# Projection and expert weights loaded a stage earlier, and the projection stage's token tiles interleaved

## The chip, the cores and the metric

The kernel runs on one NeuronCore of a Trainium2 chip. The metric is device time in microseconds from the launch's first to its last instruction; the median of several runs counts. The engines are TensorE (PE, matmuls; its weight loads are PEld), VectorE (DVE), ScalarE (ACT) and GpSimd (POOL); SP, ACT and POOL each issue transfers on a queue of their own, and all queues share 16 DMA engines. TensorE's clock is granted at one of two levels, 1.2 or 2.4 GHz; the profile writes 0.50 and 1.00.

## The reference

One decoder layer over 1024 prompt rows and 8 sequences of 8 sample rows, all in float32, width 1024:

```python
mod = jax.nn.silu(c) @ w_ada + b_ada
shift1, scale1, gate1, shift2, scale2, gate2 = jnp.split(mod[:, None, :], 6, axis=-1)
h = rmsnorm(x, norm1_g) * (1 + scale1) + shift1
aq, ak, av, mqk, mv, mo, mi, mf = jnp.split(h @ w_in, SPLITS, axis=-1)
...  # attention on aq, ak, av; short conv on mqk, then mLSTM with a carried state
mix = jnp.concatenate([hA.reshape(B, T, W_A), att.reshape(B, T, W_B)], axis=-1).astype(x.dtype) @ w_out
x = x + gate1 * mix
h2 = rmsnorm(x, norm2_g) * (1 + scale2) + shift2
x = x + gate2 * peer(h2, peer_wq, peer_keys, peer_u, peer_v)
```

`peer` scores 2 x 128 sub-keys per head, takes the 16 best experts of each of 8 heads for a row (128 picks), and sums their one-neuron outputs: u and v rows of 1024 values, gathered from a table of 16384.

## The kernel before

Three stages, each a block in which every engine has its own program; semaphores order them, and an all-engine barrier stands between stages. There is no scheduler: each engine runs its instructions in the order in which the code writes them, and an engine that waits holds back all behind it.

**Stage 0** makes the modulation rows: 12 loads of w_ada (2 MB each, two buffers, on SP's queue), 8 matmuls each, plus two tables of position biases (the second, s_bias, is written out by SP at the end). The rows go to a scratch tensor `mod_rows`.

**Stage 1** is the projection stage. Its weight w_in (14.7 MB) fills the memory from END_SMALL to END_W. Nine tiles: eight of 128 prompt rows and one of 64 sample rows. Engine programs call `tile(i, ...)` for tile 0, then in a hardware loop (Fori) for tiles 1 to 7, then for the sample tile. On TensorE a tile is: transposes of the normed rows h (L564), gates (8 columns), mqk (64 matmuls, L572), mv, two small sums of the gates (tri, all), mo, a_rep (L585), the three diag matmuls that end in m_rep (L588 to L590), the attention's q and k, scores s_ps (L598), key transposes ktok (L601), the attention's v (av), num (L613, L614), and cup, the update of the carried state (L619). Column matmuls over w_in go through `project`, so they all carry L556. Between them DVE and ACT make: x's mean square (ACT L490) and h (DVE L665, L666); the gates' log (lf); the short conv (32 DVE instructions); diag_a, diag_m, arg; decay and carry (ACT, L518, L521); og, scores, q_carry, kws (DVE, to L742), the norm of q and k (to L753, its mean square by ACT), hid and its norm, the state. POOL stores q, k, v and hid of a tile (hid to `mix_rows`, L456). ACT begins the stage by issuing w_in's eight loads and sixteen copies of 4 MB each from the old caches to the output, DRAM to DRAM:

```python
for k in range(KD):
    act.dma_start(w_in[:, k], ins["w_in"][:, k]).then_inc(sig["w_in_in"], 16)
for b in range(DB):
    for name in ("k_s", "v_s"):
        act.dma_start(outs[name][b, 0:WBUF - DS], ins["cache_" + name[0]][b, DS:WBUF]).then_inc(sig["cache_out"], 16)
```

SP meanwhile loads two mod rows, spread over 128 partitions, and then x tile by tile. Before the sample tile it reloads mod, stores the prompt's state and fetches the sample's conv_tail; after it, it stores the sample's state, and the stage ends when that has landed.

**Stage 3** first runs a sample window: attention of the 64 sample rows over the cached keys and values (POOL loads keys_t and vals), interleaved with the attention, output projection (w_out) and expert search (w_q) of prompt tile 0. SP issues the loads of w_out (4 MB) and w_q (8 MB) at that window's start. Then come nine windows of expert picks: POOL gathers one expert row per partition and pick (L1104), DVE takes the dot product, ACT the gate, TensorE the weighted sum, while the next tile's search runs between picks.

Of the kernel before, what the change touches and what calls it, by code (L numbers as in the profile page):

```python
# [19 lines left out]
P = 128  # L20
D = 1024
# [175 lines left out]
PER_P, PER_S = 59, 59  # L197
END_KEPT = W_B + N_KEPT


def layer(nc, ins, outs):

    with ExitStack() as ctx:
# [31 lines left out]
def stage0(nc, block, sig, mem, psum, const, table, ins, scratch):  # L235
# [8 lines left out]
    rows = mem[:, END_SMALL:END_SMALL + 6 * D]  # L244
    tab = mem[:, END_SMALL + 6 * D:END_SMALL + 6 * D + LTAB]
    s_part = Region(mem, END_SMALL + 6 * D + LTAB, END_W)
# [7 lines left out]
    def _(sp):  # L254
# [4 lines left out]
        for n in range(N_ADA):  # L259
# [3 lines left out]
            sp.dma_start(w[:, n % 2], ins["w_ada"][:, :, cols]).then_inc(sig[f"ada_in{n % 2}"], 16)  # L263
# [9 lines left out]
        sp.wait_ge(sig["s_bias_tab"], len(S_PIECES))  # L273
        sp.dma_start(scratch["s_bias"].ap(), s_tab).then_inc(sig["tables_out"], 16)
        sp.wait_ge(sig["tables_out"], 48)

    @block.scalar
    def _(act):
# [8 lines left out]
        nc.scalar.activation(cond, cond, ACT.Silu).then_inc(sig["cond"], 1)  # L287
        act.wait_ge(sig["small_in"], 80)
# [46 lines left out]
def stage1(nc, block, sig, mem, psum, const, ins, outs, scratch):  # L335

    w_in = mem[:, END_SMALL:END_W].rearrange("p (k n) -> p k n", k=KD)
# [30 lines left out]
    s_state = work.take(DB, H_A, DK + 1)  # L368
# [36 lines left out]
    def _(sp):  # L405
# [8 lines left out]
        with sp.Fori(1, NT) as i:  # L414
            tile(i, P, ins["x"][bass.ds(i * P, P), :])
# [23 lines left out]
        sp.dma_start(outs["m_s"], sm["mnew"][0:NS]).then_inc(sig["out1"], 16)  # L439
        sp.wait_ge(sig["s_state"], DB)  # L440
# [4 lines left out]
    def _(pool):  # L445
# [17 lines left out]
        with pool.Fori(1, NT) as i:  # L463
            store(i, P, bass.ds(i * P, P), bass.ds(i * P + WBUF - SEQ, P))
# [6 lines left out]
    def _(act):  # L471
        for k in range(KD):
            act.dma_start(w_in[:, k], ins["w_in"][:, k]).then_inc(sig["w_in_in"], 16)

# [5 lines left out]
        def tile(i, rows, kind, per):  # L480
            chain = Chain(act, sig["act1"], i * per)
# [6 lines left out]
            act.wait_ge(sig["x_in"], (i + 1) * 16)  # L488
            act.wait_ge(sig["h"], i)
            chain.link(nc.scalar.activation(squares[0:rows], x[0:rows], ACT.Square, accum_out=xss[0:rows]))  # L490
            inv_rms(xrs[0:rows], xln[0:rows], xss[0:rows], D, "x_rms")
            act.wait_ge(sig["h_t_ps"], i + 1)
            act.wait_ge(sig["av_ps"], i)
            for half in range(2):
                src = psum[:, half].rearrange("p (k t) -> p k t", k=4)[:, :, 0:rows]
                cp = nc.scalar.activation(h_t[:, 4 * half:4 * half + 4, 0:rows], src, ACT.Copy)  # L496
                cp.then_inc(sig["h_t"], 1)

# [3 lines left out]
            nc.scalar.activation(sm["soft"][0:rows], sm["soft"][0:rows], ACT.Ln, bias=1.0).then_inc(sig["soft"], 1)  # L502

# [9 lines left out]
            nc.scalar.activation(conv[:, :, 0:rows], conv_y[:, :, 0:rows], ACT.Silu).then_inc(sig["silu"], 1)  # L513

# [28 lines left out]
            assert chain.n == per, chain.n  # L543

        tile(0, P, "p", 7)
        with act.Fori(1, NT) as i:
            tile(i, P, "p", 7)
        tile(NT, NS, "s", 7)

    @block.tensor  # L550
    def _(pe):
        ident, ones = const["ident"], const["ones"]

        def project(bank, col, n, rows, at=0):
            for k in range(KD):
                mm = nc.tensor.matmul(psum[0:rows, bank, at:at + n], h_t[:, k, 0:rows], w_in[:, k, col:col + n], start=k == 0, stop=k == KD - 1)  # L556
            return mm

        def tile(i, rows, kind):
# [5 lines left out]
            tr.then_inc(sig["h_t_ps"], 1)  # L565
            pe.wait_ge(sig["h_t"], 2 * i + 2)
            pe.wait_ge(sig["w_in_in"], 16 * KD)
            pe.wait_ge(sig["mnew"], i)
            project(7, O_G, 2 * H_A, rows).then_inc(sig["gates_ps"], 1)
            for c in range(8):  # L570
                for k in range(KD):
                    mm = nc.tensor.matmul(psum[:, c // 4, c % 4 * P:c % 4 * P + rows], w_in[:, k, O_QK + c * P:O_QK + (c + 1) * P],  # L572
                                          h_t[:, k, 0:rows], start=k == 0, stop=k == KD - 1)
            mm.then_inc(sig["mqk_ps"], 1)
            pe.wait_ge(sig["scores"], i)
            project(5, O_MV, W_A, rows).then_inc(sig["mv_ps"], 1)
# [4 lines left out]
            project(6, O_MO, W_A, rows).then_inc(sig["mo_ps"], 1)  # L581

            pe.wait_ge(sig["diag_a"], i + 1)
            pe.wait_ge(sig["state"], i)
            nc.tensor.matmul(psum[0:rows, 2, 0:H_A * rows], ones[0:rows, 0:rows], diag_a_of(rows), start=True, stop=True).then_inc(sig["a_rep"], 1)  # L585
            pe.wait_ge(sig["diag_m"], i + 1)
            pe.wait_ge(sig["av"], i)
            nc.tensor.matmul(psum[0:rows, 3, 0:H_A * rows], ones[0:rows, 0:rows], diag_m_of(rows), start=True, stop=True)  # L588
# [3 lines left out]
            project(2, 0, W_B, rows)  # L592
# [1071 lines left out]
```

## Time and profile before

| | before |
|---|---|
| median of 3 runs | 4375.03 us (4374.49 to 4392.1) |
| profiled execution | 4374.66 us, span 4373.0 us |
| mean granted clock | 0.918 |
| PE busy | 3560.7 us, 81% |
| DVE busy | 2393.2 us, 55% |
| ACT busy | 1640.2 us, 38% |
| POOL busy | 1279.2 us, 29% |
| DMA | 1419.95 MB, mean 325 GB/s |

All numbers on rows are from the profiled execution. Busy shares are averages over stages with different limits, so they don't tell what bounds a stage; for that one goes by stretch, and in a stretch by the wait that ends last. A row of the timeline gives the start, the time and, in brackets, how long the engine had been idle and what released it. A float32 matmul shows as two instructions (x16 for eight matmuls).

### The profile page before, as it was taken

How to read it: one execution, taken by the hardware profiler on the slowest of the kernel's cores; microseconds unless marked ns; L12 is line 12 of the kernel's file. 1: busy time of each engine (PE TensorE's matmuls, PEld its weight loads, DVE VectorE, ACT ScalarE, POOL GpSimd, SP SyncE). 2: the span in 40 equal slices, each digit the busy share in tenths (PEclk: the TensorE clock that was granted, in tenths of full speed). 3: DMA queues.
4: the chain of work that ended last, by engine and by line, in shares of the span. 5: the costliest groups of instructions: out<-in, count | busy, mean ns of one | idle time of the engine just before them, and what ended most of it. 6: DMA issues, size and time to landing. Idle time of an engine off the chain costs nothing.

```text
span 4373.0 us, 38660 instructions
## 1 busy us (share of the span) xinstructions
PE 3560.7 (81%) x12228; PEld 1818.6 (42%) x12228; DVE 2393.2 (55%) x5587; ACT 1640.2 (38%) x4396; POOL 1279.2 (29%) x1204
## 2 busy tenths in 40 slices
PE   7288788684867987997898898789799888989877
PEld 1054454453533533443453444445345344524321
DVE  1033433322464784595486468449646845947844
ACT  0022322311335335435434533543453354334333
POOL 0000000000223343343343334234334434435433
PEclk9688888865989999999999899999999999999999
DMA  6897100146669999999999899999999999999998
GB/s 237 301 338 252 38 19 19 43 23 262 237 236 372 400 415 358 403 411 391 372 414 416 329 394 413 360 387 410 413 376 390 410 394 395 397 374 401 411 408 368
DMA packets 251979, 1419.95 MB, mean 325 GB/s; under 512 B 42963, under 2 KB 65875, under 8 KB 105603
## 3 DMA queue, kind: packets, MB, share of 16 engines
q0 software_dynamic: 168768, 1200.70, 68.4%
q1 hardware_dynamic: 79588, 132.71, 9.8%
q10 hardware_dynamic: 3440, 84.35, 5.5%
q8 instruction: 84, 1.38, 0.1%
q14 instruction: 99, 0.81, 0.1%
HBM read 1385.48 MB, written 98.73 MB: 339 GB/s over the span
## 4 chain that ended last, share of the span: by engine, by line
PE 30%; DMA 24%; DVE 11%; ACT 8%; issue 2%; POOL 0%; SPq 0%; ACTq 0%; POOLq 0%; DVEq 0%
DMA mem<-in_experts,mem 21%; PE psum L1279 20%; DVE mem L1573 6%; PE psum L1196 3%; PE psum L1178 3%; DMA mem<-key_cols 2%; ACT L1383 2%; DVE mem L1439 1%; ACT mem L1387 1%; DVE mem L1438 1%; ACT mem L1384 1%; ACT L1306 1%; PE psum L1134 1%; ACT mem L1306 1%; ACT mem L1383 1%
## 5 line engine op out<-in xcount | busy, mean ns | idle before, releaser
L1279 PE MATMUL psum<-mem 128*128 128x512 f32 (+1 forms) x4352 | 2141.1, 626 | 387.9 <-ACT mem L1387 386.4
L1104 POOL DMA_INDIRECT mem<-in_experts,mem x1088 | 1213.3, 1115 | 1872.9 <-PE psum L1279 1804.2
L1573 DVE CUSTOM_DVE_ANT_0 mem<-mem 128x1024 f32<-128x1024 f32 x1088 | 1322.8, 1222 | 708.5 <-DMA mem<-in_experts,mem 695.7
L1279 PEld LDWEIGHTS psum<-mem 128*128 128x128 f32 (+1 forms) x4352 | 776.8, 193 | 1471.1 <-ACT mem L1387 747.7
L1383 ACT ACTIVATE mem<-mem 128x1 f32<-128x1 f32 x1088 | 219.2, 201 | 1562.9 <-DVE mem L1573 1560.2
L1387 ACT ACTIVATE mem<-mem 128x128 f32<-128x128 f32 (+1 forms) x1088 | 433.3, 398 | 35.6
L556 PE MATMUL psum<-mem 128*128 128x512 f32 (+3 forms) x864 | 351.2, 558 | 10.2 <-ACT mem L496 10.2
L1384 ACT ACTIVATE mem<-mem 128x1 f32<-128x1 f32 x1088 | 320.4, 295 | 35.3
L1196 PEld LDWEIGHTS psum<-mem 128*128 128x128 f32 x2304 | 274.4, 191 | 45.2 <-issue 41.8
L1196 PE MATMUL psum<-mem 128*128 128x128 f32 (+1 forms) x2304 | 282.1, 276 | 2.5 <-ACT mem L1335 2.5
L556 PEld LDWEIGHTS psum<-mem 128*128 128x128 f32 (+1 forms) x864 | 159.7, 207 | 176.7 <-issue 162.9
L449 POOL DMA_DIRECT2D qkv_rows<-mem x9 | 5.1, 563 | 742.1 <-ACT mem L534 742.1
L564 PE MATMUL psum<-mem 128*128 128x128 f32 (+1 forms) x72 | 16.9, 415 | 192.0 <-DVE mem L666 192.0
L572 PE MATMUL psum<-mem 128*128 128x128 f32 (+1 forms) x1152 | 158.9, 310 | 0.0
L572 PEld LDWEIGHTS psum<-mem 128*128 128x128 f32 x1152 | 157.8, 226 | 0.0
L1416 DVE CUSTOM_DVE_ANT_0 mem<-psum,mem 128x128 f32<-128x128 f32 (+7 forms) x64 | 48.4, 756 | 192.7 <-PE psum L1136 166.0
L1438 DVE MAX8 mem<-mem 128x8 f32<-128x128 f32 (+3 forms) x432 | 145.8, 338 | 12.5
L1439 DVE FIND_INDEX8 mem<-mem 128x8 uint32<-128x128 f32 (+3 forms) x432 | 141.9, 328 | 0.0
L1178 PE MATMUL psum<-mem 128*128 128x512 f32 (+1 forms) x288 | 135.5, 595 | 0.0
L1134 PE MATMUL psum<-mem 64*128 64x512 f32 (+3 forms) x160 | 67.9, 531 | 56.3 <-DMA mem<-key_cols 56.2
L303 PE MATMUL psum<-mem 128*9 128x512 f32 x192 | 91.7, 637 | 20.0 <-DMA mem<-in_b_ada 13.9
L1383 ACT ACT_TABLE_LOAD x80 | 102.6, 1283 | 14.0 <-DVE mem L1573 12.6
(255 smaller groups left out, 2612.4 us busy)
## 6 DMA issues: line engine op xcount, KB each, us to landing
out_k_s<-in_cache_k ACTq DMA_DIRECT2D x8, 4080.0 KB, 125.1
out_v_s<-in_cache_v ACTq DMA_DIRECT2D x8, 4080.0 KB, 137.4
mem<-in_w_ada SPq DMA_DIRECT2D x12, 2048.0 KB
mem<-mod_rows SPq DMA_DIRECT2D x34, 512.0 KB
mem<-in_experts,mem POOLq DMA_INDIRECT x1088, 9.7
mem<-in_keys_t POOLq DMA_DIRECT2D x16, 1024.0 KB, 6.8
mem<-in_vals POOLq DMA_DIRECT2D x16, 1024.0 KB, 8.4
mem<-in_w_in ACTq DMA_DIRECT2D x8, 1796.0 KB, 24.8
```

Of the source, the lines that this page charges most:

```text
L556: mm = nc.tensor.matmul(psum[0:rows, bank, at:at + n], h_t[:, k, 0:rows], w_in[:, k, col:col + n], start=k == 0, stop=k == KD - 1)
L572: mm = nc.tensor.matmul(psum[:, c // 4, c % 4 * P:c % 4 * P + rows], w_in[:, k, O_QK + c * P:O_QK + (c + 1) * P], h_t[:, k, 0:rows], start ...
L1104: pool.indirect_dma_start(out=ring[:, g % N_SLOTS].rearrange("p a n -> p (a n)"), out_offset=None, in_=ins["experts"][:, :], in_offset=bas ...
L1178: mm = nc.tensor.matmul(psum[0:r, out_banks(n)[half]], turned[:, k, 0:r], w_out[:, k, half * 512:(half + 1) * 512], start=k == 0, stop=k = ...
L1196: mm = nc.tensor.matmul(psum[:, 5, j % 4 * P:j % 4 * P + r], w_q[:, k, j * NKEY:(j + 1) * NKEY], turned[:, k, 0:r], start=k == 0, stop=k = ...
L1279: mm = nc.tensor.matmul(psum[0:r, half], diag[:, g % 4, 0:r], ring[:, g % N_SLOTS, 1, half * 512:(half + 1) * 512], start=c == 0, stop=c = ...
L1383: chain.link(a.activation(act_v[:, c:c + 1], dots[:, c:c + 1], ACT.Gelu))
L1384: chain.link(a.activation(weight[:, c:c + 1], act_v[:, c:c + 1], ACT.Copy, scale=gate[i % 2][:, c:c + 1]))
L1387: a.activation(diag[:, g % 4, 0:r], spread, ACT.Copy, scale=weight[:, c:c + 1]).then_inc(sig["diag"], 1)
L1438: chain.link(v.max(values[:, e:e + 8], src))
L1439: chain.step(v.max_index(places[:, e:e + 8], values[:, e:e + 8], src))
L1573: v.tensor_tensor_reduce(row, row, h2[i % 2], 1.0, 0.0, ALU.mult, ALU.add, dots[:, c:c + 1]).then_inc(sig["dots"], 1)
```

## The change

Five things, in one kernel:

- w_in is loaded in stage 0 by ACT, six of its eight parts at once, two after the s_bias table has left the memory that they fill. Stage 0's own tables move behind END_W for it, and ACT, not SP, writes s_bias out. The semaphore w_in_in is kept over the barrier.
- w_ada is laid out chunk by chunk, so that a load reads 16 KB in a row for each partition instead of eight times 2 KB.
- In stage 1 the hardware loops are unrolled, and tile i+1's mean square, norm, transposes and copy to h_t are written inside tile i (`rows_rms`, `normed`, `turn`, `turned`), with a second h_t in the room of the sample's state. TensorE's order in a tile is changed.
- At the end of stage 1, SP loads w_out and w_q into w_in's place as soon as its last matmul is done, ahead of the store of the sample's state. Stage 3 loads them no more.
- Stage 3's buffers are laid out anew for that; a small copy (s_kt) is made in two parts.

```diff
-        sig.retire()
+        sig.retire(keep=("w_in_in",))
...
-        sig.retire(keep=("cache_out",))
+        sig.retire(keep=("cache_out", "w_out_in", "w_q_in"))
...
-            sp.dma_start(w[:, n % 2], ins["w_ada"][:, :, cols]).then_inc(sig[f"ada_in{n % 2}"], 16)
+            sp.dma_start(w[:, n % 2], ins["w_ada"][n]).then_inc(sig[f"ada_in{n % 2}"], 16)
...
+        for k in range(6):
+            act.dma_start(w_in[:, k], ins["w_in"][:, k]).then_inc(sig["w_in_in"], 16)
+        act.wait_ge(sig["s_bias_tab"], len(S_PIECES))
+        act.dma_start(scratch["s_bias"].ap(), s_tab).then_inc(sig["s_bias_out"], 16)
+        act.wait_ge(sig["s_bias_out"], 16)
+        act.wait_ge(sig["s_bias_ps"], len(S_PIECES))
+        for k in range(6, KD):
+            act.dma_start(w_in[:, k], ins["w_in"][:, k]).then_inc(sig["w_in_in"], 16)
...
+    def weights_in(sp):
+
+        w_out, w_q = last_weights(mem)
+        sp.wait_ge(sig["av_ps"], NT + 1)
+        sp.dma_start(w_out, ins["w_out"]).then_inc(sig["w_out_in"], 16)
+        sp.dma_start(w_q, ins["w_q"]).then_inc(sig["w_q_in"], 16)
...
         sp.dma_start(outs["m_s"], sm["mnew"][0:NS]).then_inc(sig["out1"], 16)
+        weights_in(sp)
         sp.wait_ge(sig["s_state"], DB)
...
-        for k in range(KD):
-            act.dma_start(w_in[:, k], ins["w_in"][:, k]).then_inc(sig["w_in_in"], 16)
-
+        act.wait_ge(sig["w_in_in"], 16 * KD)
...
+            if i < NT:
+                rows_rms(i + 1, P if i + 1 < NT else NS)
...
+            if i < NT:
+                turned(i + 1, P if i + 1 < NT else NS)
...
-            pe.wait_ge(sig["hraw"], i)
-            pe.wait_ge(sig["kws"], i)
+            if i >= 1:
+                pe.wait_ge(sig["ext"], i)
             for k in range(KD):
                 tr = nc.tensor.transpose(psum[:, k // 4, k % 4 * P:k % 4 * P + rows], h[0:rows, k * P:(k + 1) * P], ident[0:rows, 0:rows])
...
+            if i < NT:
+                turn(i + 1, P if i + 1 < NT else NS)
+            if i >= 1:
+                pe.wait_ge(sig["state"], i)
+            project(i, 2, 0, W_B, rows)
...
+            if i + 1 < NT:
+                normed(i + 1, P)
+            if i + 1 == NT:
+                dve.wait_ge(sig["mod_in"], 64)
+                normed(NT, NS)
...
-        dve.wait_ge(sig["mod_in"], 64)
         dve.wait_ge(sig["s_conv_in"], 16 * 8)
...
-                sp.dma_start(w_out, ins["w_out"]).then_inc(sig["w_out_in"], 16)
...
-                sp.dma_start(w_q, ins["w_q"]).then_inc(sig["w_q_in"], 16)
```

What stands where now is shown at three places. First TensorE in a prompt tile, in the program before; L564 are the transposes, L556 the projections (8 columns are the gates), L572 mqk, L579 and L580 the gates' sums, L585 a_rep, L588 to L590 the diag matmuls:

```order
L564 MATMUL psum<-mem 128x128 x8
L556 MATMUL psum<-mem 128x8 x8
L572 MATMUL psum<-mem 128x128 x64
L556 MATMUL psum<-mem 128x512 x8
L579 MATMUL psum<-mem 128x4
L580 MATMUL psum<-mem 128x4
L556 MATMUL psum<-mem 128x512 x8
L585 MATMUL psum<-mem 128x512
L588 MATMUL psum<-mem 128x512
L589 MATMUL psum<-mem 128x512
L590 MATMUL psum<-mem 128x4
L556 MATMUL psum<-mem 128x512 x16
```

The tile began with its own transposes, and q and k (the last row) followed the diag matmuls. The same place in the changed program, where L589 are the projections, L616 mqk, L598 the transposes, L633 a_rep, L638 to L640 the diag matmuls:

```order
L589 MATMUL psum<-mem 128x8 x8
L589 MATMUL psum<-mem 128x512 x8
L616 MATMUL psum<-mem 128x128 x64
L621 MATMUL psum<-mem 128x4
L622 MATMUL psum<-mem 128x4
L589 MATMUL psum<-mem 128x512 x8
L598 MATMUL psum<-mem 128x128 x8
L589 MATMUL psum<-mem 128x512 x8
L633 MATMUL psum<-mem 128x512
L589 MATMUL psum<-mem 128x512 x8
L638 MATMUL psum<-mem 128x512
L639 MATMUL psum<-mem 128x512
```

mv stands ahead of mqk, the transposes in the middle are the next tile's, and q and k stand ahead of the diag matmuls, one on either side of a_rep.

Second, ACT around the barrier between stages 0 and 1 (L225) in the program before:

```order
L285 DMA mem<-in_s_onehot 128x3864
L287 ACT_TABLE_LOAD
L287 ACTIVATE mem<-mem 128x72
L225 UNCONDITIONAL_BRANCH
L470 UNCONDITIONAL_BRANCH
L473 DMA mem<-in_w_in 128x3592 x8
L477 DMA out_k_s<-in_cache_k 64x16320
```

And in the changed one (the barrier is L230):

```order
L289 DMA mem<-in_s_onehot 128x3864
L291 ACT_TABLE_LOAD
L291 ACTIVATE mem<-mem 128x72
L293 DMA mem<-in_w_in 128x3592 x6
L295 DMA s_bias_rows<-mem 128x1288
L299 DMA mem<-in_w_in 128x3592 x2
L230 UNCONDITIONAL_BRANCH
L492 UNCONDITIONAL_BRANCH
L497 DMA out_k_s<-in_cache_k 64x16320
```

The cache copies are now the first that ACT issues in stage 1.

Third, SP at the end of stage 1 in the changed program:

```order
L458 DMA out_conv_s<-mem 128x8x3 x8
L460 DMA out_m_s<-mem 64x4
L353 DMA mem<-in_w_out 128x8192
L354 DMA mem<-in_w_q 128x16384
L463 DMA out_state_s<-mem 128x4128
```

The two weights stand between the small store m_s and the state's store; before, the state's store followed m_s, and the weights came in stage 3 behind the store of the key columns.

## Rows read from the trace of the kernel before

**Rows 1.** Busy us of each engine by stretch; last columns: PEclk, DMA share, GB/s.

```profile
0.00:146.30 146.30, 103.58 (x220) 21.66 (x220) 15.34 (x24) 1.55 (x2) 0.23 (x5) 0.91 0.62 213
1013.50:1266.90 253.40, 172.63 (x1096) 106.33 (x1096) 108.90 (x391) 73.24 (x154) 43.16 (x73) 0.82 0.66 239
1266.90:4373.00 3106.10, 2658.28 (x8264) 1276.49 (x8264) 1967.04 (x4446) 1348.31 (x3852) 1213.33 (x1088) 0.96 0.98 392
```

**Rows 2.** First and last copy issue on ACT, and all sixteen copies' landing.

```profile
150.99 0.63 ACTq L477 DMA_DIRECT2D out_k_s<-in_cache_k  x1
184.94 20.13 ACTq L477 DMA_DIRECT2D out_v_s<-in_cache_v  x1
DMA to landing us min/median/max: 49.0/130.7/216.1
```

**Rows 3.** TensorE's timeline: start, us, line, work, count, [idle before it <- releaser].

```profile
281.33 1.06 PE L619 MATMUL psum<-mem 128*128 128x129 f32 x8
376.54 1.97 PE L564 MATMUL psum<-mem 128*128 128x128 f32 x8 [12.10 <-DVE mem L666]
379.69 3.58 PE L556 MATMUL psum<-mem 128*128 128x8 f32 x16 [1.18 <-ACT mem L496]
417.97 2.08 PE L588 MATMUL psum<-mem 128*128 128x512 f32 x2 [3.43 <-DVE mem L714]
421.48 13.98 PE L556 MATMUL psum<-mem 128*128 128x512 f32 x32
```

**Rows 4.** Stretches of the second and the ninth tile, columns as before.

```profile
294.00:301.00 7.00, 5.43 (x25) 5.03 (x25) 0.34 (x1) 1.08 (x2) 0.00 (x0) 0.50 0.99 325
301.00:318.00 17.00, 17.00 (x131) 16.68 (x132) 0.84 (x3) 1.90 (x4) 0.00 (x0) 0.88 1.02 351
340.00:362.00 22.00, 22.00 (x64) 10.60 (x63) 10.62 (x12) 6.18 (x13) 0.00 (x0) 1.00 1.01 344
890.00:918.00 28.00, 28.00 (x134) 27.90 (x133) 0.31 (x2) 1.90 (x4) 0.00 (x0) 0.50 0.00 1
```

**Rows 5.** Timeline of ACT, then of DVE, behind the third tile's m_rep.

```profile
423.96 0.57 ACT L521 ACTIVATE mem<-psum 128x512 f32<-128x512 f32 x1
426.50 0.69 DVE L725 TENSOR_TENSOR mem<-mem 128x512 f32<-128x512 f32 x1
436.46 0.69 DVE L729 TENSOR_TENSOR mem<-psum,mem 128x512 f32<-128x512 f32 x1 [9.27 <-PE psum L598]
442.74 1.23 DVE L753 TENSOR_TENSOR mem<-mem 128x1024 f32<-128x1024 f32 x1
```

**Rows 6.** Landing of x asked at 212.4 and 458.6, and of mix_rows at 289.3.

```profile
DMA to landing us min/median/max: 27.8/27.8/27.8
DMA to landing us min/median/max: 3.6/3.6/3.6
DMA to landing us min/median/max: 62.7/62.7/62.7
```

**Rows 7.** What ended TensorE's idle time on the modulation matmuls (us, times).

```profile
  DMA mem<-in_b_ada: 24.9, 7
```

**Rows 8.** Timeline of TensorE, DVE and TensorE around the ninth tile.

```profile
854.87 1.06 PE L619 MATMUL psum<-mem 128*128 128x129 f32 x8
884.28 1.28 DVE L665 SCALAR_TENSOR_TENSOR mem<-mem 64x1024 f32<-64x1024 f32 x1 [19.98 <-DMA mem<-in_conv_tail]
955.73 7.08 PE L556 MATMUL psum<-mem 128*64 128x512 f32 x16
```

**Rows 9.** Chain that ended last (sample window), and the page on vals.

```profile
1029.56 13.00 DMA mem<-in_keys_t
1045.75 25.15 DMA mem<-in_vals
1150.58 5.30 DMA mem<-in_keys_t
mem<-in_vals POOLq DMA_DIRECT2D x16, 1024.0 KB, 8.4
```

More of the change, by code:

```diff
@@ L243, in stage0 @@
     rel = work.take(H_B)
-    rows = mem[:, END_SMALL:END_SMALL + 6 * D]
-    tab = mem[:, END_SMALL + 6 * D:END_SMALL + 6 * D + LTAB]
-    s_part = Region(mem, END_SMALL + 6 * D + LTAB, END_W)
+    rows = work.take(6 * D)
+    tab = work.take(LTAB)
+    w_in = mem[:, END_SMALL:END_W].rearrange("p (k n) -> p k n", k=KD)
+    s_part = Region(mem, END_SMALL + 6 * W_IN, END_W)
     s_hot, s_rel, s_tab = s_part.take(3, COLS), s_part.take(3, P), s_part.take(COLS)
@@ L413, in _ @@
         tile(0, P, ins["x"][0:P, :])
-        with sp.Fori(1, NT) as i:
-            tile(i, P, ins["x"][bass.ds(i * P, P), :])
+        for i in range(1, NT):
+            tile(i, P, ins["x"][i * P:(i + 1) * P, :])
         sp.wait_ge(sig["h"], NT)
@@ L478, in _, with rows_rms, turned, tile @@
         lnscale, eps = const["lnscale"], const["eps"]
-        def tile(i, rows, kind, per):
-            chain = Chain(act, sig["act1"], i * per)
+        chain = Chain(act, sig["act1"])
+        def rows_rms(i, rows):
+            act.wait_ge(sig["x_in"], (i + 1) * 16)
+            act.wait_ge(sig["h"], i)
+            if i >= 2:
+                act.wait_ge(sig["qss"], i - 1)
+            chain.link(nc.scalar.activation(squares[0:rows], x[0:rows], ACT.Square, accum_out=xss[0:rows]))
+            chain.link(nc.scalar.activation(xln[0:rows], xss[0:rows], ACT.Ln, scale=1.0 / D, bias=eps[0:rows]))
+            nc.scalar.activation(xrs[0:rows], xln[0:rows], ACT.Exp, scale=-0.5).then_inc(sig["x_rms"], 1)
+        def turned(i, rows):
+            act.wait_ge(sig["h_t_ps"], i + 1)
+            if i >= 2:
+                act.wait_ge(sig["av_ps"], i - 1)
+            for half in range(2):
+                src = psum[:, half].rearrange("p (k t) -> p k t", k=4)[:, :, 0:rows]
+                cp = nc.scalar.activation(h_ts[i % 2][:, 4 * half:4 * half + 4, 0:rows], src, ACT.Copy)
+                cp.then_inc(sig["h_t"], 1)
+        def tile(i, rows, kind):
             def inv_rms(out, tmp, total, n, event):
@@ L486, in inv_rms @@
                 nc.scalar.activation(out, tmp, ACT.Exp, scale=-0.5).then_inc(sig[event], 1)
[L488 to L497, printed above, removed]
             act.wait_ge(sig["gates"], i + 1)
@@ L542, in tile @@
             inv_rms(sm["hrs"][0:rows], sm["hln"][0:rows], sm["hss"][0:rows], DK, "h_rms")
[L543 to L548, printed above, removed]
+        rows_rms(0, P)
+        turned(0, P)
+        for i in range(NT):
+            tile(i, P, "p")
+        tile(NT, NS, "s")
     @block.tensor
@@ L565, in tile @@
             tr.then_inc(sig["h_t_ps"], 1)
+        def tile(i, rows, kind):
             pe.wait_ge(sig["h_t"], 2 * i + 2)
-            pe.wait_ge(sig["w_in_in"], 16 * KD)
-            pe.wait_ge(sig["mnew"], i)
-            project(7, O_G, 2 * H_A, rows).then_inc(sig["gates_ps"], 1)
+            if i == 0:
+                pe.wait_ge(sig["w_in_in"], 16 * KD)
+            else:
+                pe.wait_ge(sig["mnew"], i)
+            project(i, 7, O_G, 2 * H_A, rows).then_inc(sig["gates_ps"], 1)
+            if i >= 1:
+                pe.wait_ge(sig["scores"], i)
+            project(i, 5, O_MV, W_A, rows).then_inc(sig["mv_ps"], 1)
+            if i >= 1:
+                pe.wait_ge(sig["hraw"], i)
+                pe.wait_ge(sig["kws"], i)
             for c in range(8):
@@ L620, in tile @@
                 mm.then_inc(sig["cup"], 1)
-        tile(0, P, "p")
-        with pe.Fori(1, NT) as i:
+        turn(0, P)
+        for i in range(NT):
             tile(i, P, "p")
@@ L653, in _, with normed, tile @@
         taps = const["conv"]
-        def tile(i, rows, kind, per):
-            chain = Chain(dve, sig["dve1"], dve_base + i * per)
+        def normed(i, rows):
+            R = slice(0, rows)
+            dve.wait_ge(sig["x_rms"], i + 1)
+            if i >= 1:
+                dve.wait_ge(sig["h_t_ps"], i)
+            chain.link(v.scalar_tensor_tensor(out=h[R], in0=x[R], scalar=xrs[R], in1=mod[R, 1], op0=ALU.mult, op1=ALU.mult))
+            v.tensor_tensor(h[R], h[R], mod[R, 0], ALU.add).then_inc(sig["h"], 1)
+        def tile(i, rows, kind):
             R = slice(0, rows)
@@ L719, in tile @@
             chain.wait()
[L720 removed]
+            v.tensor_tensor(arg_of(rows), bc(const[kind + "_negT"][R], 1, H_A), heads_ps(1, rows, rows), ALU.subtract).then_inc(sig["arg"], 1)
             dve.wait_ge(sig["og"], i + 1)
@@ L779, in tile @@
                 v.tensor_tensor(state[:, 2:4], state[:, 2:4], num_ps(P, 1, (2, 3)), ALU.add).then_inc(sig["state"], 1)
-            assert chain.n == per, (kind, chain.n)
         v.memset(state, 0.0).then_inc(sig["dve1"], 1)
```

118 lines of the change are left out of this document (60 added, 58 removed).

## The prediction, on record before the changed kernel ran

> **What bounds the kernel now.** I read first the busy time of each engine by stretch [rows 1]. The modulation rows fill it to 146.3, the projection stage (eight prompt tiles, then a ninth of 64 sample rows) to 1013.5, the sample window of the expert stage to 1266.9, and 3106.1 us of expert picks the rest. In the picks the DMA engines are 98% busy at 392 GB/s: gathers bound them, and the edit moves no instruction there, so I carry them over unchanged. All that can be won lies in the first 1267 us, where a different thing ends last in each stretch.
>
> Then I read ACT's timeline behind 146.3 [rows 2]. It issues eight loads of w_in and sixteen cache copies; the last issue alone takes 20.13 us and ends at 205.07, 58.8 us into the stage. The first Square on x stands behind it, and norm, transposes and all matmuls behind that. So ACT's full issue queue holds back the stage's start.
>
> Next the TensorE timeline of a prompt tile [rows 3]. From the end of tile 0 (281.33 + 1.06 = 282.39) to that of tile 7 (854.87 + 1.06 = 855.93) seven tiles take 573.5 us, 81.93 each. TensorE stands still three times in one: 12.10 us before the transposes, 1.18 before the gates, 3.43 before diag_m; the rest, 65.2 us, is matmuls. The granted clock [rows 4] is 0.50 just after the long wait, 0.88 over the following 17 us, 1.00 late in the tile: the wait costs twice.
>
> **The tile loop, the largest term.** The new order puts tile i+1's norm, transposes and copies inside tile i, so that the 12.10 and 1.18 go. What is TensorE's work then? Transposes (1.97 us) and gates (3.43 us from 379.69 to 383.12) run at 0.50; at 1.00 they would take half, 2.7 less. The 17 us at 0.88 hold 17 x 0.12 / 0.5 = 4.1 us at half clock, 2.0 too much. diag_m and its neighbours take 3.5 us (417.97 to 421.48) for four passes of 512 columns; 32 such passes take 13.98, so 0.44 each, and 1.5 are lost. That leaves 65.2 - 6.2 = 59.0 us.
>
> What is late next is the chain DVE - ACT - DVE after m_rep, the last of the diag matmuls (421.48). Before, both q/k projections, the 13.98 us, stood behind m_rep and covered it; now they stand ahead of it, and only s_ps, the key transposes, av and num do. ACT's decay and carry end at 424.53, 3.1 us after m_rep [rows 5]; TensorE has 1.4 us for s_ps and the key transposes, so it stands 1.7 in two waits, for arg and for carry. DVE needs 5.7 us for arg and og (to 427.19), then, with no gap left in between, 7.5 for scores, q_carry, kws, the sum of squares, ACT's Ln and Exp, and the q/k norm (436.46 to 443.97): 13.2 in all. TensorE is at cup, which overwrites q and k, after 3.1 + 7.0 of av + 1.8 of num = 11.9, and stands 1.3. So 3.0 us of waits, and 62.0 per tile. Waits this short may still cost clock: the one of 3.43 us does (the 1.5 above). I take 65; bounds 62 (no loss) and 68 (all cold parts stay: 65.2 + 3.0). Seven tiles at 65 instead of 81.93 are -118.5, tile 0 gains about 1 from the order. Sum **-119** (-140 to -98).
>
> **The start of the stage.** With w_in already in memory, ACT's issues fit the queue sooner: sixteen at about 0.65 us are 10 us, and the last may wait for the first copy to land; 20 us, before 58.8. But what shares the DMA engines with what changes too. Before, the two mod rows (shift and scale, spread over 128 partitions) and the first x, three transfers of 512 KB on SP's queue, ran beside w_in and were there long before ACT was free. Now they run beside the copies from the first moment. The trace shows what that costs: x of tile 1, fetched while copies ran, landed after 27.8 us, that of tile 4, after the copies, in 3.6 [rows 6]. So 512 KB beside copies takes about 22 us once started (27.8 less some 5 of start and landing); three in line on one queue take 66, bounds 3 x 3.6 and 3 x 27.8. The first x lands some 70 us into the stage; Square, norm and transposes follow as before. 70 instead of 58.8: **+11** (-39 if only ACT's queue counts, +25).
>
> The last copy landed 216.1 us after its issue at 184.94, at 401, the first at 150.99 + 49.0 = 200 [rows 2]: 13.4 us each, 215 in all, so they still run in tile 1. There DVE waits, before it overwrites hid, for POOL's store of tile 0's hid, which took 62.7 us to land among the copies [rows 6]. It is issued some 7 us after tile 0's cup and needed 61.5 us after it: **+8** (0 to +10), once. In a tile of 82 us this was covered.
>
> **The modulation stage.** w_ada comes in 16 KB pieces per partition instead of 2 KB. TensorE waited there 24.9 us in seven waits that end with a load's last part [rows 7], the start among them. Against that, 10.8 MB of w_in now share the DMA engines with the first five loads and 3.6 MB with loads 6 and 7: at the 400 GB/s of the picks 36 us of transfer, in a stage whose DMA share is 0.62. The two about cancel. At the end s_bias no longer leaves on SP after the last row: 2 us. I take **-2** (-15 if the waits go, +8 if w_in delays the loads).
>
> **The sample tile.** Its norm waited for DVE, and DVE for the conv_tail loads, 19.98 us after its last step on the prompt state [rows 8]; TensorE stood meanwhile and then ran 28 us at 0.50 [rows 4]. From tile 7's end (855.93) to the end of av (955.73 + 7.08 = 962.81) are 106.9 us. Now x, h and the transposes are done in tile 7, so gates, mv and mqk run in those 20 us. What is late next is the same conv_tail, before DVE adds the gate bias: 8.4 us for the state + 20 + 2.4 for ACT and DVE = 30.7 until lf. Then mo at part clock (9), q (7), a_rep (0.6), k (7), diag_m, s_ps, transposes and waits (5), av (7) and two small steps: 67 to 68 us. **-39** (-41 to -30). The rest of the tile, 50 us, keeps its work. Into it come 12.6 MB of w_out and w_q, on SP's queue ahead of the state's store, which is needed 42 us after av and closes the stage. At the 392 GB/s of the picks the weights need 32 us: covered, with 10 to spare; at half that rate the end would come 22 us late.
>
> **The sample window.** In the chain that ended last, the third keys_t load took 13.00 us and the first vals 25.15, while w_out and w_q were loading; the same kind later takes 5.30, and the median of vals is 8.4 [rows 9]. 7.7 + 16.7 go: **-25** (-10 to -30; the bias rows that follow on SP's queue may be late next).
>
> Sum: -119 + 11 + 8 - 2 - 39 - 25 = -166. The profiled execution took 4374.66 us, its span 4373.0; the median of the runs is 4375.03, so no allowance is needed. 4374.7 - 166 = **4209 us**.
>
> **Rivals.** (1) x is not held up by copies and the stage starts when ACT is free: 4209 - 50 = 4159. For it: SP asks first. Against it: the landing of 27.8 us. (2) The queues take turns in larger parts, so that each of the three transfers waits for one copy of 13.4 us: x after 44 us, 4209 - 26 = 4183. Against it: a lone x would then need 13.4 + 3.6 = 17 us, the row shows 27.8. The Trainium skill (DMA: Bandwidth & Descriptors, Queues, rings and completion order) says that a DMA engine drains a whole packet of descriptors from one queue before it turns to the next; by that rule this rival would hold, and the landing here does not agree with it. (3) The tile stays at 70: cold parts remain, or another wait joins; 4209 + 7 x 5 = 4244. (4) The overlap fails, because some wait keeps one tile behind the other, and the period stays 82: 4328. Against it: no wait in the new order needs the end of the tile before, but for hraw and kws, both ready within 2 us of it. (5) Slower: TensorE never leaves the half clock in the tile loop, since no stretch of it is free of waits. Work of 59.0 us becomes 118, the period 121, the time 4209 + 7 x 56 = 4601. It turns slower than before from a period of 65 + 166/7 = 88.7. For it: in the ninth tile 64-column matmuls ran 28 us at 0.50 without a gap [rows 4]. Against it: with 128 and 512 columns every tile reaches 1.00 within some 10 us.
>
> **How the numbers follow.** Forecast 0.52, (1) 0.12, (2) 0.08, (3) 0.19, (4) 0.05, (5) 0.04. The forecast's own range is 4185 to 4235. Rivals (2) and (3) lie near it and belong to the range, (1) too; 4145 to 4258 leaves out about 0.2: (4), (5) and the tails. A difference under 0.5% (22 us) I count as none. Faster 0.94: all but (5) and part of (4); same 0.02; slower 0.04.
>
> **What would show it.** Right: a period of 62 to 69 us from cup to cup with granted clock above 0.95; the first x landing some 70 us into the stage, with ACT idle before it; one longer tile, the second; the ninth tile without the 31 us wait; the window from s_raw to the first gather near 228 us; the picks within 5 us of 3106. Wrong: ACT's issues ending last at the start; a TensorE wait above 3 us in each tile; the stage's end waiting for the state's store; picks that have changed.

## The result and the profile after

| | before | after |
|---|---|---|
| median of the runs, us | 4380.3 (4 runs, 4374.5 to 4392.1) | 4180.7 (4 runs, 4171.3 to 4189.1) |
| ratio, 95% interval | | 0.954 (0.951 to 0.957) |
| profiled execution, us | 4374.7 | 4189.1 (span 4187.3) |

The kernel became 4.6% faster, 200 us; 4209 was forecast, 28 us too much, with 4145 to 4258 as the range; it lies 4 us below the forecast's own 4185 to 4235. The two profiled executions differ by 185.7 us of span. By stage, before and after:

| from, to | before | after | measured | forecast |
|---|---|---|---|---|
| modulation stage | 146.3 | 146.0 | -0.3 | -2 |
| its end to the first Square | 58.9 | 54.2 | -4.7 | +11 |
| first transpose to tile 7's end | 643.6 | 509.5 | -134.1 | -119 + 8 |
| tile 7's end to the end of av in tile 9 | 106.9 | 66.7 | -40.2 | -39 |
| end of av to the expert stage | 50.7 | 52.3 | +1.6 | 0 |
| sample window | 253.5 | 231.8 | -21.6 | -25 |
| picks | 3106.1 | 3119.8 | +13.7 | 0 |

Between the first Square and the first transpose lie 7 us in both.

First the busy time of each engine by stretch of the kernel after, cut at the same events as [rows 1] (the columns are those of [rows 1]):

```profile
146.00:207.20 61.20, 0.00 (x0) 0.00 (x0) 3.06 (x6) 4.21 (x6) 0.31 (x1) 0.50 0.99 333
207.20:716.60 509.40, 485.07 (x2248) 310.67 (x2248) 254.40 (x602) 166.01 (x318) 18.43 (x32) 0.98 0.39 134
716.60:835.60 119.00, 88.74 (x402) 57.96 (x400) 42.25 (x120) 22.54 (x48) 3.66 (x7) 0.74 0.82 166
835.60:1067.40 231.80, 174.33 (x1096) 106.87 (x1096) 109.30 (x391) 73.43 (x155) 43.18 (x73) 0.84 0.58 207
1067.40:4187.30 3119.90, 2655.81 (x8264) 1274.90 (x8264) 1967.58 (x4446) 1348.69 (x3852) 1218.03 (x1088) 0.96 0.98 390
```

In the tile loop TensorE is busy 485 of 509 us at a granted clock of 0.98. Ahead of it lie 61 us in which it does nothing while the DMA engines are busy 0.99: that is now the longest standstill ahead of the picks. ACT's timeline there answers to [rows 2]:

```profile
146.03 0.66 ACTq L497 DMA_DIRECT2D out_k_s<-in_cache_k  x1
...
156.29 9.84 ACTq L497 DMA_DIRECT2D out_v_s<-in_cache_v  x1
200.18 1.06 ACT L508 ACTIVATE mem<-mem 128x1024 f32<-128x1024 f32 x1 [193.35 <-DMA mem<-in_x]
```

The last of the sixteen issues ends at 166.13, and ACT then waits 34 us more, for x. What ended last at the stage's start was ACT's queue and is now a DMA. TensorE's timeline of one tile in the middle of the loop answers to [rows 3]:

```profile
530.42 1.13 PE L667 MATMUL psum<-mem 128*128 128x129 f32 x8 [1.15 <-DVE mem L811]
...
580.29 0.66 PE L649 MATMUL psum<-mem 128*128 128x128 f32 x4 [0.18 <-DVE mem L778]
582.08 7.13 PE L589 MATMUL psum<-mem 128*128 128x512 f32 x16 [1.13 <-ACT mem L554]
...
592.15 1.02 PE L667 MATMUL psum<-mem 128*128 128x129 f32 x7 [1.15 <-DVE mem L811]
```

From cup to cup are 61.73 us. Three waits are left, for arg, for carry and ahead of cup for the q/k norm, 2.5 us together; the waits of 12.10 and 3.43 us are gone. One stretch differs. These are rows of DVE at the end of tile 1, whose last steps reach into tile 2, then of TensorE:

```profile
334.63 1.23 DVE L808 TENSOR_TENSOR mem<-psum,mem 128x1024 f32<-128x1024 f32 x1 [2.64 <-DMA out_v_p<-mem]
348.05 0.23 DVE L817 COPY mem<-psum 128x2 f32<-128x2 f32 x2 [10.94 <-DMA mix_rows<-mem]
```
```profile
337.26 1.13 PE L667 MATMUL psum<-mem 128*128 128x129 f32 x8 [1.89 <-DVE mem L811]
349.74 2.62 PE L616 MATMUL psum<-mem 128*128 128x128 f32 x15 [2.69 <-DVE mem L823]
```

DVE waits for tile 0's stores of v and of hid (the latter issued at 282.36, so 65.7 us in landing), and TensorE for DVE. Tiles 1 to 3 take 62.47, 66.33 and 65.09 us, 8.7 more than three others. But tile 3 has no wait beyond the usual three. These rows are the first 10 us or so of it, then tile 3 and tile 4 as windows:

```profile
405.00:415.00 10.00, 10.00 (x26) 5.48 (x26) 3.16 (x8) 6.71 (x17) 0.87 (x2) 0.66 0.39 149
403.60:468.70 65.10, 62.63 (x281) 39.67 (x281) 32.20 (x76) 21.18 (x41) 2.14 (x4) 0.95 0.09 33
468.70:530.40 61.70, 59.25 (x280) 37.92 (x281) 32.20 (x76) 21.19 (x41) 2.14 (x4) 1.00 0.10 35
```

TensorE's work takes 62.6 us in place of 59.3, at a granted clock of 0.95: right behind the two waits of 1.1 us at the end of tile 2 the clock fell to its lower level for some 7 us (an estimate: 10 us at 0.66). So 3.4 of the 8.7 us are clock, and no store. In the ninth tile the gap answers to [rows 8]:

```profile
724.60 14.51 PE L616 MATMUL psum<-mem 128*128 128x64 f32 x128
748.17 0.37 PE L621 MATMUL psum<-mem 64*64 64x4 f32 x2 [9.07 <-DVE mem L722]
...
776.29 7.08 PE L589 MATMUL psum<-mem 128*64 128x512 f32 x16 [0.74 <-ACT mem L554]
```

TensorE does gates, mv and mqk while conv_tail lands and then stands 9.07 us. In the sample window the chain that ended last reads, in answer to [rows 9]:

```profile
853.29 4.32 DMA mem<-in_keys_t
859.75 9.20 DMA mem<-in_vals
...
877.96 7.66 DMA mem<-bias_rows
899.13 7.28 DMA mem<-in_keys_t
```

The loads of 13.00 and 25.15 us are back to what they take elsewhere, and the bias rows come next.

### The profile page after: what moved, and what is told of

It is laid out like the page before. It is cut to its first block, busy times and chain, and to the rows that moved or that the text cites. A ratio compares the mean times of both kernels' runs of the same rounds, so it can differ in the third digit from the quotient of the medians.

```text
span 4187.3 us, 38259 instructions
## 1 busy us (share of the span) xinstructions
PE 3507.9 (84%) x12228; PEld 1772.0 (42%) x12228; DVE 2391.9 (57%) x5587; ACT 1616.4 (39%) x4381; POOL 1283.8 (31%) x1204
## 4 chain that ended last, share of the span: by engine, by line
PE 32%; DMA 25%; DVE 11%; ACT 8%; issue 2%; POOL 1%; SPq 0%; ACTq 0%; POOLq 0%; DVEq 0%
PE psum L1335 21%; DMA mem<-in_experts,mem 20%; DVE mem L1631 6%; PE psum L1252 4%; PE psum L1234 3%; DMA mem<-key_cols 3%; ACT L1441 2%; DVE mem L1497 1%; ACT mem L1445 1%; DVE mem L1496 1%; ACT mem L1442 1%; DMA mem<-qkv_rows 1%; ACT L1362 1%; PE psum L1190 1%; ACT mem L1441 1%
## 5 line engine op out<-in xcount | busy, mean ns | idle before, releaser
L1335 PEld LDWEIGHTS psum<-mem 128*128 128x128 f32 (+1 forms) x4352 | 774.5, 193 | 1458.0 <-ACT mem L1445 733.4
L589 PE MATMUL psum<-mem 128*128 128x512 f32 (+3 forms) x864 | 342.7, 548 | 11.0 <-ACT mem L554 9.8
L1252 PEld LDWEIGHTS psum<-mem 128*128 128x128 f32 x2304 | 274.4, 191 | 45.1 <-issue 41.7
L1252 PE MATMUL psum<-mem 128*128 128x128 f32 (+1 forms) x2304 | 282.1, 275 | 2.5 <-ACT mem L1391 2.5
L589 PEld LDWEIGHTS psum<-mem 128*128 128x128 f32 (+1 forms) x864 | 148.8, 190 | 178.4 <-issue 164.6
L616 PEld LDWEIGHTS psum<-mem 128*128 128x128 f32 x1152 | 131.5, 194 | 7.7 <-issue 4.2
L616 PE MATMUL psum<-mem 128*128 128x128 f32 (+1 forms) x1152 | 131.9, 276 | 2.7 <-DVE mem L823 2.7
L508 ACT ACTIVATE mem<-mem 128x1024 f32<-128x1024 f32 (+1 forms) x9 | 9.4, 1045 | 212.4 <-DMA mem<-in_x 212.4
```

The costliest lines, as they stand in the source:

```text
L589: mm = nc.tensor.matmul(psum[0:rows, bank, at:at + n], h_ts[i % 2][:, k, 0:rows], w_in[:, k, col:col + n], start=k == 0, stop=k == KD - 1)
L1252: mm = nc.tensor.matmul(psum[:, 5, j % 4 * P:j % 4 * P + r], w_q[:, k, j * NKEY:(j + 1) * NKEY], turned[:, k, 0:r], start=k == 0, stop=k = ...
L1335: mm = nc.tensor.matmul(psum[0:r, half], diag[:, g % 4, 0:r], ring[:, g % N_SLOTS, 1, half * 512:(half + 1) * 512], start=c == 0, stop=c = ...
```

## Experiments

Twelve kernels were run. All but one change a few lines of the changed kernel ("after" below: 4180.7 us, first gather at 1067.5). Since the picks differ from execution to execution (see the section on why), the time of the first gather is given too, which leaves them out.

**Each half by itself.** In weights_only the weights load ahead and the tile loop is that of before.

> All three weights are loaded ahead of time, but the projection stage's tile loop is that of the kernel before (no overlap of tiles, q and k projected behind the diag matmuls). My theory: the two halves add up. The start gives 4.7 us, the sample window 21.6, the loop nothing: 4380 - 26 = 4354, and the overlap's share is the other 173 of the 200 us. Rival: with w_in out of the way the copies lie beside the old tiles in another way, and the parts don't add up: more than 10 us off that number.

Measured: 4354.3 us, 0.995 (0.993 to 0.997) of before, which was 4373.6 in the runs beside it, so 19 us less (12 to 31 by the interval); first gather at 1236.3, 30.6 sooner than before. The seven tiles as windows:

```profile
278.00:851.40 573.40, 456.42 (x1963) 298.82 (x1961) 227.33 (x532) 169.51 (x301) 17.53 (x31) 0.85 0.22 77
```

They take 573.4 us, as before, at the same clock of 0.85. So the weights are worth some 20 to 30 of the 200 us and the overlap the other 170 to 180. Within the 10 us that the rival names, the parts add up.

**The weights of the expert stage.** u_wlast:

```diff
-        weights_in(sp)
...
+                sp.dma_start(w_out, ins["w_out"]).then_inc(sig["w_out_in"], 16)
...
+                sp.dma_start(w_q, ins["w_q"]).then_inc(sig["w_q_in"], 16)
```

> The loads of w_out and w_q go back to the start of the expert stage. My theory: the sample window returns from 231.8 to 253.5 us and the piece from the end of av to the stage's end gets 1.6 shorter: +20, 4201. Rival: the window got shorter from something else that the change moved (a different state of the DMA queues), and the loads are hidden either way: within 5 us of 4181.

Measured: 4203.8 us, 23 above after; ratio 0.962 (0.959 to 0.964); first gather at 1084.4, 17 later, as its tiles 1 to 3 happen to be 6.3 us shorter. The window takes 254.6 us, and its chain has the long loads again:

```profile
845.82 13.33 DMA mem<-in_keys_t
862.34 25.70 DMA mem<-in_vals
```

With the weights out of the window they are 4.32 and 9.20. The theory holds, and the rival falls.

**The weights of the projection stage.** u_win:

```diff
-        for k in range(6):
-            act.dma_start(w_in[:, k], ins["w_in"][:, k]).then_inc(sig["w_in_in"], 16)
...
-        act.wait_ge(sig["w_in_in"], 16 * KD)
+        for k in range(KD):
+            act.dma_start(w_in[:, k], ins["w_in"][:, k]).then_inc(sig["w_in_in"], 16)
```

> The loads of w_in go back to the start of the projection stage, ahead of the cache copies; all else is as in the changed kernel. My theory: what ends last at that start is whichever transfer shares the DMA engines with the first x or fills ACT's issue queue, so w_in ahead of time only changes places with the copies. The first Square then runs some 59 us into the stage, as it did before the change, in place of 54; the modulation stage is 0 to 5 us shorter without w_in's 14 MB; total within 8 us of the changed kernel's 4181. Rival: w_in's 36 us of transfer (14.4 MB at the 400 GB/s of the picks) were really taken out of the stage's start, and come back: 4210 or more.

Measured: 4174.5 us, ratio 0.953 (0.949 to 0.956): no difference from after that these runs can tell. ACT's timeline:

```profile
133.99 4.49 ACTq L489 DMA_DIRECT2D mem<-in_w_in  x8
...
173.22 16.12 ACTq L492 DMA_DIRECT2D out_v_s<-in_cache_v  x1
189.45 1.06 ACT L503 ACTIVATE mem<-mem 128x1024 f32<-128x1024 f32 x1 [182.71 <-issue]
```

The first Square waits for ACT's issues again, 55.5 us into the stage, but the stage begins at 134.0 in place of 146.0: without w_in beside them the loads of w_ada make TensorE wait 24.6 us in the modulation stage, with it 33.5. So w_in ahead costs 12 us in the modulation stage, more than the 5 expected, and at the start of the next the copies take its place. TensorE starts 10.7 us sooner than in after, but its eight tiles take 8.5 us more in this profile, and the first gather, at 1064.9, is only 2.6 sooner.

**The copies out of the way.** copies_spread issues two copies in each tile, behind the norm of the next; no_copies leaves them out:

```diff
-        for b in range(DB):
+        def copies(b):
...
                 rows_rms(i + 1, P if i + 1 < NT else NS)
+                copies(i)
```

> The sixteen cache copies are no longer issued all ahead of the first Square, but two in each tile, behind the Square of the next tile. My theory: what ends last at the stage's start is the landing of the first x beside the copies, and the tiles 1 to 3 are 8.6 us longer because of the stores that land among the copies. The first Square then runs some 8 us into the stage in place of 54, all tiles take 61.7 to 63 us, and the time falls by 46 + 7 = 50 to 55 us, to 4128. Rival: the copies need the same bandwidth wherever they stand, so each tile's own loads and stores are late in its place: within 15 us of 4181.

> The cache copies are left out (the old rows of k_s and v_s are not written), to see what the stage is like with no other traffic. My theory: the first x lands within 10 us of the stage's start, TensorE starts some 46 us sooner, no tile is longer than 63 us; about 4126. Rival: TensorE's start is held by ACT or by the norm even so, and gains less than 20 us.

Measured: copies_spread 4127.4 us, ratio 0.945 (0.942 to 0.948), first gather at 1009.0; no_copies 4108.8 in one run, first gather at 1010.2. The first Square of each:

```profile
155.80 1.06 ACT L508 ACTIVATE mem<-mem 128x1024 f32<-128x1024 f32 x1 [149.08 <-DMA mem<-in_x]
```
```profile
154.20 1.06 ACT L505 ACTIVATE mem<-mem 128x1024 f32<-128x1024 f32 x1 [147.56 <-DMA mem<-in_x]
```

Spread copies cost as little as none: up to the first gather the two agree within 1.3 us. Against after, TensorE starts 44.4 us sooner and the eight tiles lose 7.3 less. With spread_spaced (below) this is the fastest kernel that computes everything, 53 us below after (42 by the two ratios to before, since the runs of before beside it were 7 us faster).

**What slows x: the length of the copies or their pieces?** small_pieces:

```diff
+        for b in range(2):
+            for name in ("k_s", "v_s"):
+                to = outs[name][b, 0:WBUF - DS].rearrange("(g h r) n -> h g (r n)", h=2, r=4)
...
+        act.wait_ge(sig["x_in"], 16)
+        for b in range(2, DB):
```

> The copies of the first two sequences are issued in 8 KB pieces in place of large ones, and those of the other six only when the first x has landed. The bytes that share the DMA engines with x are of the same kind, only the pieces are smaller. My theory: the DMA engines turn from queue to queue by piece, so a transfer of 4 KB pieces is slowed by the size of the pieces beside it: the first x lands 13 to 20 us into the stage in place of 53. Rival: the queues share the bandwidth evenly whatever the size of the pieces; then x still lands 40 us or more into the stage, or as soon as these four copies are through.

Measured: ACT's next issue behind its wait for x is at 172.72, 20.9 us into the stage (151.79), so x had landed by then. But twelve more issues kept ACT to 200.3, the first Square came at 200.4, and the one run took 4167.4. Since the transfers were shorter as well as their pieces, this did not settle the question, and a pair was run that differs in the pieces alone, with a fill on GpSimd that marks x's landing:

```diff
-                    to = outs[name][b, 1020 * h:1020 * h + 1020]
...
+                    to = outs[name][b, 0:WBUF - DS].rearrange("(g h r) n -> h g (r n)", h=2, r=4)[h]
```

> The copies of the first four sequences are issued as two halves each (sixteen transfers of 2040 KB, in large pieces as before), those of the other four when the first x has landed; GpSimd's first fill waits for x and so marks its landing. It is a pair with the next run, which differs only in the size of the pieces. Theory: the DMA engines turn from queue to queue piece by piece, so the length of a transfer is nothing to x, and it lands about 53 us into the stage, as beside whole copies. Rival: they drain one queue's whole transfer before they turn; then half the length gives half the wait, and x lands 20 to 31 us in (three turns of 6.7 us, and three times at most 3.6 for its own).

> The same transfers of 2040 KB, each in pieces of 8 KB. Theory: x lands 8 to 15 us into the stage, as the pieces beside its own are an eighth as long. Rival: as in its pair, 20 to 31 us, since the transfers are as long as there; or, if the queues share the bandwidth evenly, as late as beside large pieces.

Measured, half_large: its fill, and ACT's queue (q10) from 146 to 206 us (records, MB, share of the DMA engines; each piece is a record, and so are the few bytes that end a transfer):

```profile
193.91 0.31 POOL L481 MEMSET mem<- 128x256 f32 x1 [193.46 <-DMA mem<-in_x]
```
```profile
q10 hardware_dynamic: 397, 17.63, 86.5%
```

The same of half_small, with two of ACT's issues:

```profile
159.59 0.31 POOL L481 MEMSET mem<- 128x256 f32 x1 [159.13 <-DMA mem<-in_x]
```
```profile
q10 hardware_dynamic: 2201, 17.12, 80.1%
```
```profile
149.31 2.35 ACTq L501 DMA_DIRECT2D out_k_s<-in_cache_k  x2
...
170.65 15.63 ACTq L501 DMA_DIRECT2D out_k_s<-in_cache_k  x2
```

With stage starts at 148.51 and 149.29, x lands 45 us in beside large pieces and 10 beside small ones, while as many bytes pass in the same time. So a transfer in small pieces is slowed by the size of the pieces beside it, and the queues do not share by bytes. The turns themselves can be counted in after, where SP's queue (q1) brings the mod rows and x in 384 pieces of 4 KB. First from 146 to 148.8 us, where ACT's queue has no record yet, then both queues from 150 to 190:

```profile
q1 hardware_dynamic: 102, 0.42, 49.2%
```
```profile
q10 hardware_dynamic: 240, 12.53, 91.5%
q1 hardware_dynamic: 240, 0.92, 7.9%
```

One record of either queue passes for one of the other, a copy's 65 KB for 4 KB of x. 45 is less than the 53 expected and far above the rival's 31. That too fits turns by record: until x is through, the copies' queue moves 288 records of 15.67 MB in after (148.8 to 197 us) and 304 of 13.58 MB in half_large (151.4 to 193.5); at 65 KB a piece, 48 of the first and 96 of the second are small, because half copies end twice as often. The Trainium skill (DMA: Bandwidth & Descriptors, Queues, rings and completion order) has an engine drain a packet of descriptors from a queue before it turns. That the pieces set the wait agrees with it; that a turn ends with a transfer, as the forecast's rival read it, does not (45 against 20 to 31). By the counts a turn takes one record here. Small pieces are no way out: ACT is busy with issues to 246 us, and the one run took 4210.9 (half_large: 4180.5).

**All copies behind the first norm.** copies_behind:

```diff
-        for b in range(DB):
-            for name in ("k_s", "v_s"):
...
         rows_rms(0, P)
+        for b in range(DB):
+            for name in ("k_s", "v_s"):
...
         turned(0, P)
```

> All sixteen copies in one go as in the changed kernel, but behind the norm of tile 0 and ahead of the copies of its transposed rows. My theory: x then lands some 8 us into the stage and the first Square starts as with the spread copies, but ACT's issues of the sixteen take 20 us, as they did from 146 to 166, and the transposed rows wait behind them: some 15 us lost again at tile 0, and some 9 in tiles 1 to 3 to stores that land among the copies. 4127 + 24 = 4151. Rival: only the landing of x mattered, and the issues of the copies hide behind TensorE's other work: 4136 or less.

Measured: 4162.8 us, ratio 0.949 (0.946 to 0.953), 12 above the theory. ACT, then TensorE at the end of tile 2:

```profile
166.06 9.26 ACTq L577 DMA_DIRECT2D out_v_s<-in_cache_v  x1
175.37 1.09 ACT L516 ACTIVATE mem<-psum 128x512 f32<-128x512 f32 x2 [17.50 <-issue]
```
```profile
383.96 1.41 PE L667 MATMUL psum<-mem 128*128 128x129 f32 x5 [20.45 <-DVE mem L811]
```

The issues hold the transposed rows until 175.4, as expected (TensorE stands 13.9 us for them). The miss is in tile 2: it takes 81.0 us, since the tiles now run some 45 us earlier against the same copies (tile 1 ends 146.5 us behind the first issue, in after 191.2), and DVE waits 21.2 us there for tile 1's store of v. That step was taken over from after as 9 us and is 24 over tiles 2 and 3 (4.2 of it in tile 3, which has only the usual waits but a clock of 0.93).

**w_in without the copies.** u_win_spread is u_win with the copies spread:

> The loads of w_in go back to the start of the projection stage, and the copies are spread as two per tile. My theory: with the copies gone from the start, w_in ahead of time is worth something, but less than its 36 us of transfer: the modulation stage again ends at 134 us in place of 146, the first x lands soon, and the gates of tile 0 wait for the last part of w_in, at 134 + 37 = 171, against some 165 with w_in ahead. So 5 to 10 us slower than the spread copies alone: 4134. Rival: the prefetch gives all of its transfer time, 36 less the 12 that it costs before: 4151 or more. Second rival: nothing is lost, at most 4127.

Measured: 4135.9 us, ratio 0.946 (0.941 to 0.950). The stage begins at 130.6, and TensorE's first gates are these:

```profile
173.71 13.25 PE L585 MATMUL psum<-mem 128*128 128x8 f32 x32 [14.41 <-DMA mem<-in_w_in]
```

In copies_spread they start at 165.97: w_in ahead is worth 7.7 us here. Tile 7 ends 7.1 later without it and the first gather 13.3; the other 6.2 lie in the sample tile and the sample window, whose code is the same in both. The medians differ by 8.5, but their intervals overlap; what speaks for the theory is the place in the trace.

**Spaced loads of w_in.** spread_spaced is copies_spread with:

```diff
         for k in range(6):
+            act.wait_ge(sig["mod_row"], k + 1)
             act.dma_start(w_in[:, k], ins["w_in"][:, k]).then_inc(sig["w_in_in"], 16)
```

> The copies are spread as two per tile, and besides the first six parts of w_in are asked for one after each modulation row in place of all at the start. My theory: in the modulation stage the first loads of w_ada share the DMA engines with 10.8 MB of w_in, and TensorE waits 9.4 us there for the third; spaced out, the stage gets 5 to 10 us shorter, on top of the spread copies: 4120. Rival: the stage is bound by the sum of its bytes, so spacing moves the wait to later rows: as with the spread copies alone, 4128.

Measured: 4128.4 us, ratio 0.944 (0.942 to 0.945): the rival. TensorE's waits in the modulation stage (us, times, longest):

```profile
PE psum L316 <- DMA mem<-in_norm_gain: 13.8, 3, 8.3
PE psum L316 <- DMA mem<-in_b_ada: 13.0, 5, 4.7
PE psum L309 <- DMA mem<-in_rel: 11.9, 1, 11.9
```

They are 38.7 us in nine waits, in copies_spread 34.0 in six. The longest wait for a later load goes from 9.7 to 8.3, and others join it.

**The order of q and k.** qk_behind puts both projections behind the diag matmuls, as before, and keeps the overlap:

```diff
-            project(i, 2, 0, W_B, rows)
...
+            project(i, 2, 0, W_B, rows)
+            project(i, 3, W_B, W_B, rows).then_inc(sig["qk_ps"], 1)
```

> The projections of q and k go back behind the diag matmuls, and the overlap of the tiles stays. My theory: the order of q and k matters, because with them ahead the 14 us cover DVE's work on the gates before diag_m; behind, TensorE waits 3 to 6 us before diag_m in each tile, and loses some clock with it, but need no longer wait for arg, carry and the q/k norm, or does so before cup: a period of about 66 in place of 61.7, +35 us, 4216. Rival: waits change places, one for one: within 10 us of 4181.

Measured: 4215.1 us, ratio 0.964 (0.962 to 0.967), 34 above after, and the first gather is 35.6 later; the period alternates between 66.0 and 67.1. The one wait of its tile:

```profile
592.22 2.08 PE L636 MATMUL psum<-mem 128*128 128x512 f32 x2 [5.65 <-DVE mem L772]
```

5.65 us stand in place of 2.5; of the 4.9 us that a tile is longer, the other 1.7 go with the clock, 0.96 over these tiles against 1.00 in an undisturbed tile.

## Why the prediction came out as it did

**The tile loop** was right in its mechanism and 23 us short in size. The step that was off is the choice of 65 between 62 and 68 for the period: it added 3 us to every tile for clock lost in short waits, argued from a wait of 3.43 us. An undisturbed tile takes 61.74. The waits were placed right (arg, carry, cup; 2.5 us against 3.0), and 59.3 us of work stand against 59.0. What the rows of before couldn't show is that waits of 1.1 us cost clock only now and then: the granted clock over the last four prompt tiles (468.7 to 715.6) is 1.00, but tile 3, with the same waits, lost 3.4 us to it. Tiles 1 to 7 of the eleven profiles with this order hold 71 with no wait above 1.2 us; 60 of them ran at 1.00, eleven at 0.92 to 0.97, 1.7 to 5.4 us longer, two of these right behind a wait of over 5 us. What decides it is not shown. So the 3 us were right for some tiles and were charged to all. In qk_behind, with 5.65 us of wait, every tile is at 0.95 to 0.97.

**The start of the stage** was named right (x among the copies, with ACT idle before it) and mis-sized by 16 us, with the wrong sign for the term: +11 forecast, -4.7 measured. The step that failed is "three in line on one queue take 66", 22 each. The first Square came 54 us in, 18 for each of the three. The 66 let all three run beside copies from their first byte; by the counts above, 102 of their 384 pieces were through before the copies' first record, and only the rest went one for one with the copies. At the forecast's 22 us for 128 pieces these 282 take 48 us, and with its 5 us for start and landing that makes 53 (an estimate). x of tile 1, alone in the queue and with copies under way from its start, again took 28 (asked for at 207.2, Square at 235.2), as in [rows 6]. Rivals (1) and (2) fall: x is held up by the copies, and a turn takes one record and not a whole copy. That 4180.7 lies so near to rival (2)'s 4183 is luck: by that rival x comes after 44 us, and it came after 54.

**The store of hid** was forecast at +8 in tile 1's place. Of the 8.7 us over three tiles 5.3 go with stores, of v in tile 1 (0.7) and of hid in tile 2 (4.6: a wait of 2.7 and a lower clock behind it); the 3.4 of tile 3 are clock alone. What these three tiles lose is no fixed sum: beside as many bytes of copies 2.4 in u_wlast, 12.8 in u_win (clock among it), nothing in half_large, and 24 in copies_behind, where the tiles run earlier.

**The modulation stage** came out at -0.3. "The two about cancel" is what the experiments show: with the new layout of w_ada, s_bias off SP's queue and no w_in beside them the stage ends at 134.0 and 130.6 (two profiles), 12 to 16 us sooner than before; with w_in it ends at 146.0 to 151.8 (ten profiles).

**The sample tile** (-40.2 for -39), **the sample window** (-21.6 for -25, and u_wlast gives 22.7 back) and the bias rows as the next to be late are as forecast; w_out and w_q did not reach the state's store.

**The picks** took 13.7 us more in the profiled execution. Over the fourteen profiled executions, whose gathers there are the same, they take 3096.8 to 3121.0, and before's 3106.1 lies between, so this is within chance, though the forecast had named 5 us. Without them the two profiles differ by 199.4, the medians by 199.6.

In sum the tile loop and the stage's start missed by -23 and -16 us, the other terms by +5 together: -200 in place of -166. Of these 34 us the time shows 28, as the median of before is 5.6 higher here than the profiled execution that the sum started from. Rival (3), a period of 70, (4) and (5) fall with the period of 61.7.

## What to carry to other kernels

A prefetch is worth what is late next at the place it leaves, not the transfer's time: w_in ahead bought nothing while sixteen copies stood behind it, and 8 us at TensorE's start when they were spread. Bulk copies that nobody waits for belong in the loop's idle DMA time, a few per tile, and not ahead of the first load of a stage; moving them took two lines and gave a fifth to a quarter of what the whole change gave. When tiles overlap, order the producer's work so that each chain across engines is covered by matmuls that need nothing from it; here the place of two projections was worth 4.9 us a tile.

## What the runs showed of the hardware

A load of 512 KB, third in its queue, lands 45 us into the stage beside copies in pieces of 65 KB and 10 us beside as many bytes in pieces of 8 KB: the DMA engines turn between the queues of SP and ACT record by record (240 against 240 in 40 us of after). ACT's issues stall sooner with many pieces: fifteen whole copies in large pieces are issued in 0.6 to 1.1 us each and the sixteenth takes 9.84, while two half copies in small pieces take up to 15.6. And beside two waits of 1.1 us in a tile of 62 TensorE's granted clock was 1.00 in 60 of 71 tiles and 0.92 to 0.97 in eleven; beside one wait of 5.65 us it was 0.95 to 0.97 in all seven.
